# Second mixer of a two-layer trunk: compact inverse in 32-column tiles, mean-free v, decays from running sums, one written order per engine

## Chip, cores and metric

One core of a Trainium2 chip. The metric is the device time of one execution, in microseconds; the runs shown before the change are three of the same program.

## What is computed

A causal two-layer trunk on 512 tokens of width 1024, in f32: layer 0 has a gated linear attention and a spatial gating unit, layer 1 an RWKV-7 time mixing and a Conformer convolution; each layer ends in an output projection and a squared-ReLU MLP. The change is in layer 1. Of the reference, what matters:

```python
# RWKV-7, heads of 64 channels
h = h + (token_shift(h) - h) * mu
r, k, v, xw, xa, xg = split(h)
decay = exp(-exp(-softplus(-(w0 + tanh(xw) @ w2)) - 0.5))
a = sigmoid(a0 + xa @ a2);  g = sigmoid(xg) @ g2
kk = heads(k * k_k);  kk = kk / max(norm(kk), 1e-12)
k = k * (1 + (a - 1) * k_a)
# S_t = S_{t-1} (diag(decay_t) - kk_t^T (kk_t * a_t)) + v_t^T k_t ;  y_t = S_t r_t
y = scan(r, decay, k, v, kk, a)
y = (y - mean(y)) * rsqrt(var(y) + 64e-5) * gn_g + gn_b      # per head
y = (y + sum(r * k * r_k) * v) * g
# Conformer: z = a * sigmoid(gate); 31-tap causal depthwise conv + bias; LayerNorm; silu
```

## The kernel before

Everything is channel-major: a tile holds 128 channels on the partitions and 512 tokens in the columns. f32 matrix products with weights are made of three f32r products: weights and activations are cut into a high part (ScalarE: `w_hi`, line 720 in this stage) and a rest (GpSimd: `w_lo`, line 501), and every one of the eight k-steps of an output tile takes three matmuls of 512 columns (`tile`, line 861). Weights come in chunks of two tiles, double-buffered; SP loads chunk n once the rest of chunk n-2 is made, ScalarE cuts it once TensorE is through with chunk n-2.

The second mixer has 22 input tiles (`ROWS`): 14 go through the token shift (`evac_a`, `evac_q`, `evac_b`: psh by VectorE, dsh by ScalarE, the mix by VectorE into kx, vT, rx, low0 or low1), 8 are values and gates of the convolution. Then four channel blocks c = 0..3 of two heads each, in four time chunks of 128:

- `zw`, `za`: two products of 512 columns give the decay and a. `decay`: a running sum over each chunk (line 1670), the sum less its value at the middle (1673) and less the step itself (1678) by VectorE, three exponentials of 128x512 by ScalarE (739, 742, 744).
- `ksq`, `ks`, `kn`: norm of kk. `dyn`: eight VectorE steps that make AR (two parts: kk and r, decayed), bT and kT. `bonus` (line 1158).
- `scores`: for each of the 8 pairs yy of chunk and head four products in a bank, which VectorE copies under a mask into SC; then the start X, XT of the inverse, and three transposes into vtok, btok, ktok.
- The inverse of a triangular 128x128 matrix for each yy, by doubling: level lv = 1..6 has `tx` (line 1204: SC with one half of X, 64 columns; ScalarE copies it to TX, line 772) and `dx` (line 1219: TX with XT, and 1216: XT with TX; VectorE copies both under masks into X and XT, lines 1756 and 1758). Each is done in two halves b of four yy. X, XT and TX are full 128x128 although only blocks along the diagonal are in use until the last level.
- State, per chunk n: `g` (1234, 1238), `u` (1246), `st` (state 1256 and 1258, output y 1263 to 1267), with copies by ScalarE (G line 777, U line 781) and VectorE (Sp line 1779).
- `post`: y less its head mean (a product with BLK of 512 columns, line 1275, and a VectorE step), variance (1280), root, spread (1288), gain and gn_b by ScalarE, bonus and gate by VectorE.
- `taps`: 31 VectorE steps per block on cv (line 1807), each on the result of the one before; then `conv_ln`, and the output projection `out` (1327), which needs m_hi and m_lo of every block.

The order of all of this is one list, `ORDER1`, made by loops: the slices (quarters of an input tile, two k-steps each) are put between the steps of a block by the tables `FILL`, `SCORE_N`, `LEVEL_N`, `STATE_N`, the taps by `LEVEL_TAPS`, and the evacuation of a tile stands right behind its last slice. Each engine walks through this same list and does its own part of each step; nothing within one engine overtakes. At the start of the kernel, VectorE makes byte masks from `masks_f`.

Of the kernel before, what the change touches and what calls it, by code (L numbers as in the profile page):

```python
# [8 lines left out]
SEQ = 512  # L9
FF = 4 * D  # L10
P = 128
KD = D // P
TT = SEQ // P
# [3 lines left out]
CT = 4  # L17
# [3 lines left out]
COLUMN_HALVES = [slice(0, 64), slice(64, 128)]  # L21

# [29 lines left out]
for _name, _n, _times in [("gla", 128, 2), ("score", 256, 2), ("reset64", 128, 4), ("reset128", 128, 4)] \  # L52
        + [(f"lvl{a}{lv}", 64, 4) for lv in range(LEVELS) for a in ("X", "XT")]:
    MSRC[_name] = (sum(n for _, n in MSRC.values()), _n)
    MCOLS[_name] = (sum(n for _, n in MCOLS.values()), _n * _times)
# [4 lines left out]
def build(nc, xT_in, weights, cols_in, mats_in, masks_in, sgu_ln_in, sgu_w_in, alpha_w_in, low_w_in, out):  # L60
# [5 lines left out]
    with ctx:  # L66
# [24 lines left out]
        before_stages = sb("before_stages", [P, 56])  # L91
# [69 lines left out]
        with ExitStack() as own:  # L161
# [21 lines left out]
            t_a = sb("t_a", [P, SEQ])  # L183
# [5 lines left out]
            zpad = sb("zpad", [P, SEQ + TAPS - 1])  # L189
            sgate = dsh  # L190
# [12 lines left out]
            c_norm = sb("c_norm", [P, TT])  # L203

# [35 lines left out]
        def half_of(t, b, B, side):  # L240

            v = t[:, :, :].rearrange("p y (q h b) -> p (y q) h b", h=2, b=B)
            q = P // (2 * B)
            return v[:, 4 * b * q:4 * (b + 1) * q, side, :]

        def half_of_one(t, yy, B, side):
            return t[:, yy, :].rearrange("p (q h b) -> p q h b", h=2, b=B)[:, :, side, :]

# [36 lines left out]
        DYN = ["at", "ab", "ak", "bt", "k2", "kt", "rt", "rk"]  # L285
        POST = ["yc", "yrs", "yn", "yb", "ym"]
        LN = ["st", "mv", "rs", "scaled", "gain"]

# [42 lines left out]
        def quarters(tiles):  # L331
            return [("slice", t, q) for t in tiles for q in range(4)]

        def taps_in(c, counts):
            ends = [sum(counts[:i + 1]) for i in range(len(counts))]
            return [[("taps", c, e - n, e)] if n else [] for n, e in zip(counts, ends)]

        ORDER1 = [("slice", t, q) for q in range(4) for t in (0, 2)] + [("stat",)] + quarters([4]) + [("spread",)] \
            + quarters([3])[:2] + [("zw", 0)] \
            + quarters([3])[2:] + [("za", 0), ("decay_v", 0, 0), ("ksq", 0)] \  # L340
            + [("decay", 0, 1), ("decay_v", 0, 1)] + quarters([14])[:1] + [("ks", 0), ("ks_v", 0), ("decay", 0, 2)] \
            + [("decay_v", 0, 2), ("kn", 0), ("kn_v", 0)] + quarters([14])[1:] + [("dyn", 0, 0)] \
            + [("dyn", 0, 1)] + quarters([15])[:3] + [("bonus", 0), ("slice", 15, 3)]
        FILL = {0: [5, 7, 6, 1, 16, 17], 1: [8, 10, 9, 18, 19], 2: [11, 13, 12], 3: [20, 21]}

        SCORE_N = {0: [1] * 6, 1: [1] * 6, 2: [1, 1, 1, 1, 0, 1], 3: [2, 2, 1, 1, 1, 1]}
        LEVEL_N = {0: [1] * 6, 1: [1] * 6, 2: [1, 1, 1, 1, 0, 0], 3: [0] * 6}
        STATE_N = {0: [2, 1] * 4, 1: [1] * 8, 2: [1, 0, 1, 0, 1, 0, 0, 0], 3: [0] * 8}
        LEVEL_TAPS = {0: [5, 5, 2, 4, 1, 2, 3], 1: [5, 5, 2, 2, 1, 1, 3], 2: [5, 5, 2, 2, 1, 1, 3],
                      3: [1, 3, 5, 2, 5, 4, 5]}  # L350
        for c in range(CT):
            gaps = quarters(FILL[c])

            def fill(n):
                took = gaps[:n]
                del gaps[:n]
                return took
# [21 lines left out]
            for i in range(6):  # L379
                ORDER1 += [("scores", c, i)] + fill(SCORE_N[c][i])  # L380
# [1568 lines left out]
```

## Time and profile before

| | us |
|---|---|
| median of 3 runs (lowest to highest) | 1389.52 (1388.11 to 1390.04) |
| profiled execution | 1388.51 |
| its span, first to last instruction | 1386.7 |
| busy over the span: PE, PEld | 1279.2, 1038.0 |
| DVE, ACT, POOL | 682.2, 421.6, 518.6 |

PE is TensorE, PEld its weight loads, DVE VectorE, ACT ScalarE, POOL GpSimd. Matmul records overlap and their ends are modelled: what a stream of matmuls costs is read from start to start, and the busy time of a stretch counts overlap once. Idle time is read together with what ended it.

### The profile page before, as it was taken

How to read it: one execution, taken by the hardware profiler on the slowest of the kernel's cores; microseconds unless marked ns; L12 is line 12 of the kernel's file. 1: busy time of each engine (PE TensorE's matmuls, PEld its weight loads, DVE VectorE, ACT ScalarE, POOL GpSimd, SP SyncE). 2: the span in 40 equal slices, each digit the busy share in tenths (PEclk: the TensorE clock that was granted, in tenths of full speed). 3: DMA queues.
4: the chain of work that ended last, by engine and by line, in shares of the span. 5: the costliest groups of instructions: out<-in, count | busy, mean ns of one | idle time of the engine just before them, and what ended most of it. 6: DMA issues, size and time to landing. Idle time of an engine off the chain costs nothing.

```text
span 1386.7 us, 21884 instructions
## 1 busy us (share of the span) xinstructions
PE 1279.2 (92%) x9060; PEld 1038.0 (75%) x9060; DVE 682.2 (49%) x992; ACT 421.6 (30%) x536; POOL 518.6 (37%) x374
## 2 busy tenths in 40 slices
PE   5999999999999999979798888787899999999997
PEld 4797978888888888856666656564688888888885
DVE  7435365551124444457758587675655511244334
ACT  4547333221122222253334324222432211222110
POOL 4341435554445555431121030110245544455541
PEclk9899999999999999989999999897999999999998
DMA  4331212222322223210011010000022232222221
GB/s 183 115 107 46 77 72 96 91 91 100 112 91 91 91 91 105 101 67 32 32 34 50 11 50 14 31 33 1 28 95 91 91 105 108 91 91 91 94 88 61
DMA packets 16808, 105.74 MB, mean 76 GB/s; under 512 B 1872, under 2 KB 2144, under 8 KB 4832
## 3 DMA queue, kind: packets, MB, share of 16 engines
q1 hardware_dynamic: 16304, 104.03, 21.1%
q8 instruction: 58, 0.95, 0.3%
q10 hardware_dynamic: 432, 0.64, 0.1%
q14 instruction: 14, 0.11, 0.0%
HBM read 102.57 MB, written 2.10 MB: 75 GB/s over the span
## 4 chain that ended last, share of the span: by engine, by line
issue 50%; PE 27%; POOL 21%; DVE 1%; DMA 0%; POOLq 0%; ACT 0%; SPq 0%; DVEq 0%
PE ps L861 23%; POOL w_lo L501 21%; PE ps L946 3%; PE ps L915 1%; DMA w_raw<-in_weights 0%; DVE x L1361 0%; PE ps L896 0%; POOL w_lo L490 0%; POOLq L495 0%; ACT w_hi L601 0%; POOLq L498 0%; SPq L454 0%; DVE xsq L1372 0%; DVE scaled L1431 0%; DVE x L1433 0%
## 5 line engine op out<-in xcount | busy, mean ns | idle before, releaser
L501 POOL TENSOR_TENSOR w_lo<-w_raw,w_hi 128x512 fp32r<-128x512 f32 x368 | 509.6, 1415 | 827.5 <-ACT w_hi L514 284.1
L861 PE MATMUL ps<-h_hi,w_hi 128*128 128x512 f32 x696 | 283.7, 408 | 11.6 <-POOL w_lo L490 11.6
L861 PE MATMUL ps<-h_lo,w_hi 128*128 128x512 f32 x696 | 275.0, 395 | 0.0
L861 PE MATMUL ps<-h_hi,w_lo 128*128 128x512 f32 x696 | 274.8, 395 | 0.0
L861 PEld LDWEIGHTS ps<-h_hi,w_hi 128*128 128x128 f32 x696 | 132.8, 191 | 51.3 <-issue 12.2
L589 ACT ACTIVATE w_hi<-w_raw 128x2048 fp32r<-128x2048 f32 x50 | 95.7, 1914 | 194.7 <-PE ps L861 143.4
L861 PEld LDWEIGHTS ps<-h_hi,w_lo 128*128 128x128 f32 x696 | 132.8, 191 | 28.7
L861 PEld LDWEIGHTS ps<-h_lo,w_hi 128*128 128x128 f32 x696 | 133.3, 192 | 25.9 <-issue 0.5
L861 PE MATMUL ps<-f_hi,w_lo 128*128 128x512 f32 x384 | 149.5, 389 | 0.0
L861 PE MATMUL ps<-f_hi,w_hi 128*128 128x512 f32 x384 | 149.5, 389 | 0.0
L861 PE MATMUL ps<-f_lo,w_hi 128*128 128x512 f32 x384 | 149.5, 389 | 0.0
L1403 DVE TENSOR_TENSOR f_hi<-relu 128x512 f32 x64 | 56.8, 888 | 154.7 <-ACT relu L564 152.8
L564 ACT ACTIVATE relu<-ps 128x512 f32<-128x512 f32 x56 | 33.5, 598 | 223.4 <-PE ps L861 223.4
L1807 DVE SCALAR_TENSOR_TENSOR cv<-zpad,cols,cv 128x512 f32<-128x512 f32 x120 | 99.3, 827 | 3.2
L514 ACT ACTIVATE w_hi<-w_raw 128x2048 fp32r<-128x2048 f32 x32 | 61.1, 1909 | 80.0 <-PE ps L861 56.9
L861 PEld LDWEIGHTS ps<-f_hi,w_hi 128*128 128x128 f32 x384 | 72.1, 188 | 15.0
L861 PEld LDWEIGHTS ps<-f_hi,w_lo 128*128 128x128 f32 x384 | 72.1, 188 | 14.9
L1421 DVE TENSOR_TENSOR scaled<-ps,rn 128x512 f32<-128x512 f32 x16 | 11.1, 691 | 146.7 <-PE ps L861 112.1
L861 PEld LDWEIGHTS ps<-f_lo,w_hi 128*128 128x128 f32 x384 | 72.1, 188 | 14.8
L990 PE MATMUL ps<-w_hi,h_hi 128*128 128x256 f32 x256 | 76.4, 298 | 2.7 <-POOL w_lo L493 2.1
L990 PE MATMUL ps<-w_lo,h_hi 128*128 128x256 f32 x256 | 74.0, 289 | 0.0
L990 PE MATMUL ps<-w_hi,h_lo 128*128 128x256 f32 x256 | 73.9, 289 | 0.0
(305 smaller groups left out, 1941.9 us busy)
## 6 DMA issues: line engine op xcount, KB each, us to landing
w_raw<-in_weights SPq DMA_DIRECT2D x93, 1024.0 KB, 4.9
outT<-x SPq DMA_DIRECT2D x8, 256.0 KB, 2.0
x<-in_xT SPq DMA_DIRECT2D x6, 256.0 KB, 7.3
masks_f<-in_masks SPq DMA_DIRECT2D x1, 768.0 KB, 10.6
x<-in_xT ACTq DMA_DIRECT2D x2, 256.0 KB, 5.6
w_raw<-in_weights SPq DMA_DIRECT2D x1, 512.0 KB, 6.4
low_w<-in_low_w SPq DMA_DIRECT2D x1, 512.0 KB, 11.3
sgu_ln<-in_sgu_ln SPq DMA_DIRECT2D x1, 512.0 KB, 3.6
```

The lines of the kernel that those rows point to most:

```text
L501: piece = pool.tensor_tensor(w_lo[:, j, at], w_raw[:, j, at], w_hi[:, j, at].bitcast(f32), SUB)
L514: act.activation(w_hi[:, n % 2, :], w_raw[:, n % 2, :], ACT.Copy).then_inc(s("hi_done"), 1)
L564: act.activation(relu[:, g % 2, :], bank(g % 2), ACT.Relu).then_inc(s("relu_done"), 1)
L589: act.activation(w_hi[:, n % 2, :], w_raw[:, n % 2, :], ACT.Copy).then_inc(s("hi_done"), 1)
L861: mm = pe.matmul(bank(gb(g) if isinstance(i, int) else g % 2), w, r, start=(k == 0 and m == 0), stop=(k == K - 1 and m == 2))
L915: mm = pe.matmul(bank(gb(gu + t)), w, r, start=(k == 0 and m_ == 0), stop=(k == KD - 1 and m_ == 2))
L946: mm = pe.matmul(bank((gd + j) % 2), w, r, start=(k == 0 and m_ == 0), stop=(k == HALF_K - 1 and m_ == 2))
L990: mm = pe.matmul(tok_bank(g), a, b, start=(k == 0 and m == 0), stop=(k == KD - 1 and m == 2))
L1403: tt(f_hi[:, bass.ds(4 * i + c, 1), :].rearrange("p a n -> p (a n)"), relu[:, g % 2, :], relu[:, g % 2, :], MUL).then_inc(s("fhi_done"), 1)
L1421: tt(scaled[:, j, :], bank((gd + j) % 2), rn[:, :], MUL)\
L1807: stt(cv[:, c, :], zpad[:, j:j + SEQ], col("conv_w", TAPS * c + j), cv[:, c, :], MUL, ADD)\
```

## The change

- *Inverse.* X, XT and TX become `xc`, `xtc`, `txc` of 64 columns per yy, which hold only the two 64x64 diagonal blocks. Levels 1 to 5 run as four tiles of 64 rows and 32 columns of weights (`QUARTERS`) with 32 moving columns; `dx` (for X) and `dxt` (for XT) are steps of their own, `dxt` for all eight yy at once; VectorE copies X in halves of 128 columns and XT once per level in 256. Level 6 makes only the block off the diagonal: 64 columns, copied by ScalarE into `txc` and XT; ScalarE also copies the diagonal blocks into XT (`xt_diag`). Banks alternate by level.
- *Scores.* The products of the two heads alternate, so that neighbours use different halves of the partitions.
- *Mean-free v.* v is transposed by a product with `CEN` (identity less the head mean), so y comes out without its mean; the mean product and its step go; gain and gn_b are part of VectorE's steps.
- *Decays.* The running sum has a zero in front of each chunk (129 columns), and ScalarE makes the three exponentials straight from it, in pieces of 128x128 with the middle as bias; t_c's and t_b's VectorE steps go. The step with k_a moves to ScalarE (`ak`, into `t_g`).
- *Room.* Two buffers each for dsh and zpad; the gate uses zpad itself.
- *Order.* `ORDER1` and the loops that make it go. Three lists are written out, `PE1` (443 steps), `DVE1`, `ACT1`, one per engine, with single k-steps for quarters, single taps, `s` and `y` for `st`.
- *Start of the kernel.* The masks have 1025 columns for 1536, made into bytes by 12 steps for 18. The clearing of SC and others stands ahead of the norm.

```diff
-            X = sb("X", [P, 8, P])
             XT = sb("XT", [P, 8, P])
-            TX = sb("TX", [P, 8, P])
+            xc = sb("xc", [P, 8, 64])
+            xtc = sb("xtc", [P, 8, 64])
+            txc = sb("txc", [P, 8, 64])
...
+            def exps(c):
+                act.wait_ge(s("cum_done"), c + 1)
...
+                for dst, first, i, name, last in ((t_b, 0, 0, "ea_done", "at"), (t_c, 1, 1, "en_done", "kt"),
+                                                  (t_d, 1, 0, "ep_done", "rt")):
+                    if c:
+                        act.wait_ge(*dyn_step(last, c - 1))
...
+                    for n in range(TT):
+                        one = act.activation(dst[:, n * P:n * P + P], cum[:, n, first:first + P], ACT.Exp,
+                                             bias=mid[:, i, n:n + 1], scale=(-EXP_HALF, EXP_HALF)[i])
+                    one.then_inc(s(name), 1)
...
+                    for lhs, at in ((bT, slice(0, 256)), (kT, slice(256, 512))):
+                        for h2, r in enumerate(COLUMN_HALVES):
+                            ar = AR[r, c % 2, i, :, :].rearrange("p a n -> p (a n)")
+                            mm = pe.matmul(bank(5 + h2, at.start, at.stop), lhs[r, i * P:i * P + P], ar,
+                                           start=True, stop=True)
...
+                        for r, to in QUARTERS:
+                            mm = pe.matmul(as2(ps[to, tx_bank(lv, b), 32 * at:32 * at + 32], B), SC[r, yy, to],
+                                           side_of_one(xc, r, yy, B, 0), start=True, stop=True)
...
+                        for r, to in QUARTERS:
+                            w = slice(to.start - r.start, to.stop - r.start)
+                            mm = pe.matmul(as2(ps[to, x_bank(lv, b), 32 * at:32 * at + 32], B), xtc[r, yy, w],
+                                           side_of_one(txc, r, yy, B, 0), start=True, stop=True)
...
+            def dxt(c, lv):
...
+                for yy in range(8):
+                    for r, to in QUARTERS:
+                        w = slice(to.start - r.start, to.stop - r.start)
+                        mm = pe.matmul(as2(ps[to, xt_bank(lv), 32 * yy:32 * yy + 32], B), txc[r, yy, w],
+                                       side_of_one(xtc, r, yy, B, 1), start=True, stop=True)
...
+                    if b == 0:
+                        mm = pe.matmul(to, one, CEN[:, :], start=True, stop=True)
...
-                    pe.matmul(bank(7), BLK, y[:, :], start=True, stop=True).then_inc(s("ymean_mm"), 1)
...
-                    tt(t_c[:, :].rearrange("p (n t) -> p n t", t=P), b3, b3[:, :, 63:64].broadcast_to([P, TT, P]), SUB)\
...
-                    tt(t_b[:, :], t_c[:, :], t_a[:, :], SUB).then_inc(s("ca_done"), 1)
```

A stretch of the new list of TensorE, block 3, which has no slices left:

```diff
+            ("scores", 3, 4), *run("slice", 21, 5, 8), ("conv_mean", 0), *run("tok_tr", 3, 0, 3), ("tx", 3, 1, 0),
+            ("tx", 3, 1, 1), ("dx", 3, 1, 0), ("dx", 3, 1, 1), ("dxt", 3, 1), ("tx", 3, 2, 0), ("tx", 3, 2, 1),
+            ("post", 2, 0), ("dxt", 3, 2), ("dx", 3, 2, 0), ("dx", 3, 2, 1), ("tx", 3, 3, 0), ("tx", 3, 3, 1),
...
```

## Rows read from the trace of the kernel before

**Rows 1.** Stretches: length; busy time of PE, PEld, DVE, ACT, POOL; clock, DMA share, GB/s.
```profile
576.20:629.00 52.80, 42.81 (x239) 32.14 (x237) 26.75 (x50) 23.11 (x32) 15.96 (x12) 0.90 0.20 73
629.00:719.90 90.90, 78.37 (x977) 58.60 (x976) 62.33 (x100) 30.71 (x57) 16.80 (x12) 0.94 0.10 36
719.90:808.80 88.90, 76.31 (x1005) 55.82 (x1003) 64.17 (x100) 31.10 (x57) 18.10 (x12) 0.94 0.11 37
808.80:891.80 83.00, 66.13 (x957) 47.59 (x955) 62.10 (x100) 29.52 (x55) 11.16 (x8) 0.92 0.08 25
891.80:963.40 71.60, 57.10 (x883) 42.50 (x884) 50.20 (x88) 18.70 (x40) 4.99 (x4) 0.93 0.05 18
963.40:989.00 25.60, 21.57 (x242) 15.93 (x238) 8.97 (x17) 10.04 (x17) 0.00 (x0) 0.80 0.00 1
...
629.00:645.20 16.20, 15.95 (x113) 11.22 (x112) 11.12 (x18) 6.49 (x10) 5.00 (x4) 1.00 0.18 66
911.40:941.20 29.80, 22.06 (x599) 18.84 (x598) 26.10 (x48) 9.36 (x20) 4.99 (x4) 1.00 0.11 37
```

**Rows 2.** Waits of PE, second mixer: us in total, times, longest.
```profile
PE ps L1204 <- DVE XT L1758: 22.0, 21, 5.7
```

**Rows 3.** Timeline before the first score product: start us, us, engine and line, [idle before].
```profile
614.13 0.75 DVE L1691 SCALAR_TENSOR_TENSOR t_f<-kx,cols,ps 128x512 f32<-128x512 f32 x1 [2.14 <-PE ps L1152]
620.52 0.69 DVE L1631 TENSOR_TENSOR dsh<-rn,ps 128x512 f32<-128x512 f32 x1 [5.64 <-PE ps L861]
...
626.56 1.13 PE L1158 MATMUL ps<-rx,mats 128*128 128x512 f32 x2 [1.99 <-DVE rx L1721]
```

**Rows 4.** Timeline of PE, short products, K*M of the weights, columns.
```profile
629.01 0.71 PE L1172 MATMUL ps<-AR,bT 64*128 64x256 f32 x4
...
639.81 0.70 PE L1178 MATMUL ps<-bT,AR 64*64 64x64 f32 x32
640.44 0.50 PE L861 MATMUL ps<-h_hi,w_hi 128*128 128x512 f32 x1
...
641.01 0.39 PE L861 MATMUL ps<-h_hi,w_lo 128*128 128x512 f32 x1
641.24 0.40 PE L861 MATMUL ps<-h_hi,w_hi 128*128 128x512 f32 x1
...
645.21 1.16 PE L1204 MATMUL ps<-X,SC 128*64 128x64 f32 x32
646.30 1.12 PE L1130 MATMUL ps<-low,low_w 32*128 32x512 f32 x2
...
648.94 0.34 PE L1216 MATMUL ps<-TX,XT 128*64 128x64 f32 x4
...
650.76 0.29 PE L1219 MATMUL ps<-XT,TX 128*64 128x64 f32 x4
...
751.28 0.43 PE L1280 MATMUL ps<-mats,ysq 128*32 128x2 f32 x32
751.64 0.50 PE L861 MATMUL ps<-h_hi,w_hi 128*128 128x512 f32 x1
```

**Rows 5.** Groups of VectorE, second mixer: busy us, mean ns | idle before.
```profile
L1807 DVE SCALAR_TENSOR_TENSOR cv<-zpad,cols,cv 128x512 f32<-128x512 f32 x120 | 99.3, 827 | 3.2
...
L1758 DVE COPY_PREDICATED XT<-masks,ps 128x256 f32<-128x256 uint8 x48 | 22.9, 483 | 0.6 <-PE ps L1219 0.6
...
L1756 DVE COPY_PREDICATED X<-masks,ps 128x256 f32<-128x256 uint8 x40 | 20.0, 500 | 27.5 <-PE ps L1219 27.5
```

**Rows 6.** Groups of ScalarE, second mixer.
```profile
L742 ACT ACT_TABLE_LOAD x4 | 5.1, 1283 | 0.1
...
L777 ACT ACTIVATE G<-ps 128x128 f32<-128x128 f32 x16 | 4.4, 274 | 46.9 <-PE ps L1238 46.9
...
L815 ACT ACTIVATE cv<-cv,cols 128x512 f32<-128x512 f32 x4 | 2.9, 802 | 0.0
...
L827 ACT ACTIVATE m_hi<-ym 128x512 fp32r<-128x512 f32 x4 | 2.5, 620 | 0.0
```

More of the change, by code:

```diff
@@ L21 @@
 COLUMN_HALVES = [slice(0, 64), slice(64, 128)]
+QUARTERS = [(h, slice(a, a + 32)) for h in COLUMN_HALVES for a in (h.start, h.start + 32)]
 MIX0 = [1, 4, 4, 2, 2, 4, 4, 4, 4, 4, 4]
@@ L326, in build @@
         TOK = {"v": (v_tok, 1), "sv": (sv, 5), "u": (u_tok, 7), "g": (g_tok, 9)}
[L331 to L343, printed above, removed]
@@ L399, in build, with run @@
[L399 to L403 removed]
+        def run(name, *a):
+            return [(name, *a[:-2], k) for k in range(a[-2], a[-1])]
@@ L1317, in out_, with conv_mean, conv_var @@
-            def out_(t, a, b):
-                n, g = N_OUT1, FIRST_TILE[N_OUT1] + t
-                if a == 0:
+            def conv_mean(c):
+                pe.wait_ge(s("tap_done"), TAPS * (c + 1))
+                if c == 0:
+                    pe.wait_ge(s("score_done"), 8 * CT)
+                mm = pe.matmul(bank(6), ONES, cv[:, c, :], start=(c == 0), stop=(c == CT - 1))
+                if c == CT - 1:
+                    mm.then_inc(s("cmean_mm"), 1)
+            def conv_var(c):
+                pe.wait_ge(s("csq_done"), c + 1)
+                if c == 0:
+                    pe.wait_ge(s("conv_step"), CT)
+                for n in range(TT):
+                    for q in range(0, P, 32):
+                        mm = pe.matmul(ps[q:q + 32, 6, n:n + 1], (t_f, t_b, t_d, t_e)[c][:, n * P + q:n * P + q + 32],
+                                       ONES[:, 0:1], start=(c == 0 and n == 0), stop=(c == CT - 1 and n == TT - 1))
+                mm.then_inc(s("cvar_mm"), 1)
@@ L1328, in out_ @@
-                if b == KD:
+                k = M_TILES[i]
+                pe.wait_ge(s("m_lo_done"), 8 + i + 1)
+                for m, (w, r) in enumerate(cuts(n % 2, t * KD + k, k, M_HI1[k], M_LO1[k])):
+                    mm = pe.matmul(bank(g % 2), w, r, start=(i == 0 and m == 0), stop=(i == KD - 1 and m == 2))
+                if i == KD - 1:
                     mm.then_inc(s("gemm_done"), 1)
             steps = {"slice": slice_, "stat": lambda: stat(2), "spread": lambda: spread(2), "zw": zw, "za": za, "ks": ks, "kn": kn,
-                     "bonus": bonus, "scores": scores, "tx": tx, "dx": dx, "g": g_, "u": u_, "st": st, "post": post, "conv_ln": conv_ln, "out": out_}
@@ L1663, in decay @@
[L1663 to L1681 removed]
+                    dve.wait_ge(s("psh_zero"), 1)
@@ L1827, in m @@
                 tt(M_LO1[k], M_SRC1[k], F(M_HI1[k]), SUB).then_inc(s("m_lo_done"), 1)
-            steps = {"stat": start, "spread": started, "evac_a": evac_a, "evac_b": evac_b, "decay_v": decay, "ks_v": ks, "kn_v": kn, "dyn": dyn, "bonus": bonus, "scores": scores,
-                     "dx": dx, "st": st, "post_v": post, "taps": taps, "conv_ln": conv_ln, "m": m}
-            for name, *a in ORDER1:
+            steps = {"stat": lambda: norm(2), "zero": zero, "evac_a": evac_a, "evac_b": evac_b, "scan": scan, "dec": dec_,
+                     "ks_v": ks, "kn_v": kn, "dyn": dyn, "bonus": bonus, "scores": scores, "dx": dx, "dxt": dxt, "s": s_,
+                     "post_v": post, "tap": tap, "conv_sub": conv_sub, "conv_root": conv_root, "conv_scale": conv_scale, "m": m}
+            for name, *a in DVE1:
                 if name in steps:
```

847 lines of the change are left out of this document (490 added, 357 removed), and 27 rows, old and new, of tables (ACT1, PE1).

## The prediction

> **What bounds the kernel now.** I read three kinds of view, in this order. First the table of stretches [rows 1]: the second mixer runs from 576.2 to 989.0 us of a span of 1386.7 us, 412.8 us, and the change touches next to nothing outside it. The columns to look at are those of TensorE (busy 42.81, 78.37, 76.31, 66.13, 57.10 and 21.57 us, 342.3 together), of VectorE (274.5) and of ScalarE (143.2), and the granted clock, under 1.00 in all six stretches. So TensorE is the bound, but an imperfect one: for 70.5 us it stands, and in part of the rest it is at 1.2 GHz, the lower of its two levels. The cuts are the first score product of each channel block (629.0, 719.9, 808.8, 891.8), the last state product (963.4) and the last step of `out` (989.0).
>
> Second, for whom TensorE waits [rows 2]: 22.0 us in 21 waits go to L1204 (`tx`, the first product of a level) behind L1758, VectorE's last copy of the level before. Why such a copy is late is seen in the timeline [rows 3]: after t_f at 614.13 VectorE stands for 5.64 us, since the next step in the one common order is the evacuation of tile 14 (L1631); the eight steps of `dyn` behind it could have run, and the bonus product comes only at 626.56. The order sets this, no resource does.
>
> Third, the timeline of the short products [rows 4]. An f32 product leaves two records. `tx` takes 1.09 us for both halves (645.21 to 646.30), the 64 records of `dx` 1.94 us (648.94 to 650.88, 0.12 us for each group of four), one f32 product of 512 columns 1.12 us with its drain (646.30). A matmul of a slice follows the last after 0.23 us (641.01, 641.24), so a k-step is 0.68.
>
> **TensorE, part by part.** (a) *Compact inverse.* Now five levels of 1.09 + 1.94 and a last one with half the `dx`, 2.06: 17.2 us a block, 69 us in four. After: 64 + 64 + 64 records a level, 64*32 tiles with 32 columns, 960 in five levels; the last level has 64 records with 64 columns on two column tiles. No row has 64*32 with 32 columns. From above: L1178, four tiles of 64*64 with 64 columns, 32 records in 0.63 us (639.81 to 640.44), 19.7 ns. From below: a quarter of the 29 ns of a `dx` record, half the columns on twice the tiles, 7.3 ns. L1280 has the width of 32 and four column tiles, but 2 columns: 32 records in 0.36 us (751.28 to 751.64), 11.3 ns [rows 4]. It is the nearest, so I take 12 ns: 11.5 us, plus 64 x 0.029 = 1.9, is 13.4 us a block. Saved: 3.8 us a block, 15 in four; by the bounds from 33 saved to 14 lost.
>
> Records with 2 columns start 11.3 ns apart and those with 64 columns 19.7 ns [rows 4]. Against this change speaks the Trainium skill, TensorEngine Tiling (Array Packing), Performance Considerations: one column takes as long as 60, and no tiling factor should be taken from a dimension that is small already. The two rows do not bear that out for four tiles side by side, and by L1280's row the time is 1313.7; by the page it would be that of the second rival, 1343.
>
> (b) *Scores.* The first four records of a pair of heads take 0.71 us with their drain (629.01), all eight 1.07. With the two halves of the partitions in turn they can run two at a time. I take 0.86 (between 0.53 and 1.07): 0.2 x 16 = 3.4 us saved. (c) *Mean-free v.* Four 512-column mean products over y go, 4 us; the centring rides on transposes of v that are there anyway. (d) *Finer steps.* Counted in the two orders, slices stand in 65 unbroken runs before and in 65 after, so changes between the two kinds of product cost the same.
>
> **The other engines.** VectorE [rows 5]: t_c, t_b, t_e and one step on y go, sixteen steps like the 0.69 of L1631 [rows 3], 11 us. X copies go from 256 to 128 columns: 40 x 0.50 becomes 40 x 0.35 (between 0.25 and 0.50), 6 us. XT copies of the same size fall from 48 to 20, at 0.483: 13.5 us. Level 0 saves 1. Together 31 us: 274.5 becomes 243, 55 to 60 of it in each block. ScalarE [rows 6]: three exponentials per block in 12 pieces of 128x128 at 0.274 (3.3 us), for three steps of 128x512 like the 0.620 of L827 (1.9 us); t_g, two diagonal and two last copies of XT, +2.6; smaller level copies and the two steps on y that go, -2. That is 2 us a block more; it stays the idlest of the three, but its queue matters: the writer of t_b, t_c and t_d waits for at, kt and rt of the block before, and behind it stand `tx` copies for which TensorE waits at `dx`. POOL's work per chunk is unchanged (67.0 busy of 412.8), and its weights come as before, per chunk. At the start of the kernel the masks shrink (512 KB for 768, 12 casts for 18). Nothing in the first products reads them; I take 0. Six casts fewer, none dearer than the 0.483 of L1758, would save up to 3 us if nothing hid them, and a layout that moves costs 1 at most.
>
> **The sum, stretch by stretch.** Each is TensorE's new work over the share in which it is busy, or VectorE's, or the chain, whichever is longest. TensorE's share is 86% in block 0 now and 98% where slices stand between all short steps (629.0 to 645.2) [rows 1]; I take 92%. VectorE is at 88% at its densest (911.4 to 941.2), and I take that. The few us "from the clock" are a choice: at 0.93 to 0.94 some 10 us of a block are at the lower level, and shorter waits give part of them back.
> - Up to the first score: TensorE has 46 k-steps of 0.68 and 6 us of short work, 37 us. In the chain to the bonus product `spread` comes six k-steps sooner (4 us), the 5.64 us go, one table load of 1.28 us goes, the exponentials cost 1.4 more, and t_c and t_b go (1.4). That is 11 us, and one more for the hand-overs of the steps that go; 52.8 becomes 41.
> - Block 0: 78.4 - 3.8 - 0.9, + 0.7 (51 k-steps for 50), - 2 from the clock: 72; over 0.92, 78 for 90.9.
> - Block 1: 76.3 - 3.8 - 0.9 - 1.0, + 2.7 (44 k-steps for 40), - 2: 71; 77 for 88.9.
> - Block 2: 66.1 - 5.7 - 2 = 58; 63 for 83.0. VectorE, 62.1 - 8 = 54 over 0.88, 61, is just under it.
> - Block 3: 11 k-steps for 16, and VectorE binds: 50.2 - 8 + 5 (six taps of block 2 fall here now, 0.827 each) = 47; over 0.88, 53, and some 5 from the last tap to the last state product: 58 for 71.6.
> - Tail: y 1.5; square and copy 1.2; variance, root, reciprocal 0.9; a table 1.28; four silu and cuts of 0.80 + 0.61, 5.6; the last cut and rest 1.3; six matmuls 1.6; hand-overs 1: 14.5. With out steps that come late, 20 for 25.6.
>
> 41 + 78 + 77 + 63 + 58 + 20 = 337 for 412.8: 75.8 us less, of which 22 are work and the rest waiting and clock. The profiled execution took 1388.51 us, 1.8 of it outside the span; the median of 1389.52 lies 1.0 above it, so 1389.5 - 75.8 = 1313.7.
>
> **Rivals.** *The waits stay.* The new lists are fixed; if steps end later than they were written for, each in-order queue hands its delay on and TensorE idles as now. Then only the work goes: 1389.5 - 22.4 = 1367. For it: the three queues have to agree through 443 steps of TensorE alone. Against it: today's idle times are at places that the new lists visibly fill. 12%.
> *The tiles give nothing.* A record of 32 columns holds its tile as long as one of 64, so it costs the 19.7 ns of L1178: 14 us lost for 15 saved, 1343. For it: both ends of my bound have 64 columns; against it: L1280. 7%. It is the rule of TensorEngine Tiling (Array Packing) in the Trainium skill.
> *Denser than I take.* 98% everywhere and a clock near 1.00: 315 us for the stage, 1292. 10%.
> *Slower.* `exps` is one block of 12 x 0.274 us, three small ones and a table load, 5.2 us in ScalarE's queue between `tx` copies, with cuts of the weights beside it, while TensorE stands at `dx` in its own fixed order. The mean wait at `tx` is 22.0/21 = 1.05 us now, the longest 5.7 [rows 2]. With 24 levels the gain is gone from 3.2 us of added waiting a level on; at 3.5 it is 1389.5 - 75.8 + 84 = 1398. Only three such blocks stand inside levels: 3%.
>
> **Numbers.** The forecast has 68% (its own bounds: 1297 to 1339), the rivals 12, 7, 10 and 3. The range of 1294 to 1346 leaves out the first rival, the last, and half of the denser one, 20%. About 0.2% (2.8 us) is what a measurement of this kernel can tell from no change: faster 0.96, same 0.01, slower 0.03.
>
> **What would show it.** A stage near 337 us in which TensorE idles 30 to 40 us; records of `tx`, `dx` and `dxt` some 12 ns apart (20 by the second rival); under 10 us of waits at `tx`; VectorE and not TensorE dense in block 3; the bonus product of block 0 near 614. I am wrong if TensorE still idles 70 us, if VectorE's copies of 128 columns cost what those of 256 do, if ScalarE becomes what TensorE waits for most, or if a stage outside the second mixer moves by more than 1 us.

## The result, and the profile after

The changed kernel takes 1351.59 us (median of 4 runs, 1345.29 to 1354.03) where the kernel before takes 1389.47 (1388.11 to 1390.04) beside it: a ratio of 0.9717, 95% interval 0.9696 to 0.9738. Its profiled execution took 1352.92 us, with a span of 1351.1. I had said 1313.7, with 1294 to 1346 as the range. The gain is 38 us where I had put 76: the sign was right, the size was half, and the range missed.

The table of stretches of the changed kernel, cut as [rows 1]: first score product of each block, last state product, end of the stage. Columns: length, then busy time and records of TensorE, its weight loads, VectorE, ScalarE and GpSimd, the granted clock, DMA share, GB/s. The last line is the whole stage.

```profile
core 0: us, PE busy (x) PEld busy (x) DVE busy (x) ACT busy (x) POOL busy (x), PEclk, DMA share, GB/s
577.30:619.30 42.00, 40.03 (x233) 29.82 (x231) 22.90 (x51) 25.33 (x44) 12.88 (x11) 0.96 0.18 67
619.30:707.20 87.90, 73.58 (x1433) 54.06 (x1433) 50.98 (x87) 29.65 (x66) 18.14 (x14) 0.90 0.15 50
707.20:790.50 83.30, 74.23 (x1534) 52.46 (x1532) 53.68 (x95) 35.58 (x78) 12.35 (x10) 0.98 0.08 28
790.50:860.40 69.90, 59.17 (x1405) 42.72 (x1402) 41.50 (x75) 26.37 (x63) 8.14 (x7) 0.85 0.10 33
860.40:937.60 77.20, 60.57 (x1520) 43.32 (x1518) 51.88 (x90) 21.27 (x48) 10.88 (x8) 0.73 0.09 30
937.60:953.20 15.60, 15.60 (x107) 11.85 (x104) 9.12 (x16) 8.72 (x13) 0.00 (x0) 0.91 0.01 2
...
577.30:953.20 375.90, 323.19 (x6217) 234.23 (x6215) 230.06 (x412) 146.92 (x311) 62.40 (x48) 0.88 0.11 38
```

The stage takes 375.9 us for 412.8; I had 337. Block 3 is the odd one: 77.2 us, longer than the 71.6 of before [rows 1], at a granted clock of 0.73, where I had forecast 58. TensorE's work fell by 19.1 us and its idle time from 70.5 to 52.7. I had written that it would idle 30 to 40 us; the 337 itself leaves room for some 23 only (342.3 of work, less 22.4 saved, less 6 for the clock, is 314).

Who TensorE waits for, over the stage (us in total, times, longest). At the head of this view of before stood steps of other engines. Behind the 22.0 us of [rows 2] came:

```profile
PE ps L1152 <- DVE k_norm L1687: 9.7, 4, 4.7
PE ps L1256 <- ACT U L781: 8.9, 7, 5.0
PE ps L1234 <- DVE Sp L1779: 8.1, 9, 3.0
```

In the changed kernel:

```profile
PE ps L1397 <- issue: 14.4, 9, 3.0
PE ps L1381 <- issue: 7.9, 7, 1.8
PE ps L1359 <- issue: 5.2, 3, 2.3
PE ps L1425 <- ACT G L905: 3.0, 8, 0.4
PE ps L992 <- issue: 2.9, 1, 2.9
PE ps L1413 <- DVE Sp L1985: 2.6, 5, 0.6
PE ps L1464 <- issue: 2.4, 1, 2.4
```

The waits for other engines, on which my whole argument turned, are as good as gone: the largest is 3.0 us. In their place stand 33 us of "issue", time in which TensorE waits for nothing that the profile shows: at L1397 (`dxt`), L1381 (`dx`), L1359 (`tx`), at L992, a weight slice whose operands had long been there, and at L1464 (the sum of squares in `post`). By engine, the named waits are 10.9 us for ScalarE and 7.0 for VectorE; before they were 18.7 and 51.9.

Two of these pieces in the timeline of TensorE in block 0 (start, length, what, and in brackets the idle time ahead of it), with two groups that run without a pause ahead of them:

```profile
640.67 0.76 PE L1397 MATMUL ps<-xtc,txc 64*32 64x32 f32 x64
641.28 0.41 PE L1381 MATMUL ps<-txc,xtc 64*32 64x32 f32 x26
...
645.68 0.46 PE L1381 MATMUL ps<-txc,xtc 64*32 64x32 f32 x32
645.96 0.48 PE L1397 MATMUL ps<-xtc,txc 64*32 64x32 f32 x32
648.70 0.64 PE L1397 MATMUL ps<-xtc,txc 64*32 64x32 f32 x30 [2.25 <-issue]
649.10 0.24 PE L1359 MATMUL ps<-xc,SC 64*32 64x32 f32 x1
649.10 0.24 PE L1397 MATMUL ps<-xtc,txc 64*32 64x32 f32 x2
649.15 1.05 PE L1359 MATMUL ps<-xc,SC 64*32 64x32 f32 x63
650.16 0.65 PE L1381 MATMUL ps<-txc,xtc 64*32 64x32 f32 x32
653.76 0.79 PE L992 MATMUL ps<-h_hi,w_hi 128*128 128x512 f32 x1 [2.95 <-issue]
```

The first piece lies in the middle of one step: `dxt` issues its 64 records with no wait among them, and 32 run before the pause and 32 behind it. Between the two pauses run 30 + 1 + 2 + 63 + 32 = 128 records. The trace has 127 weight loads and one entry of the sequencer beside them, 256 instructions together. The table of DMA queues has a queue of kind "instruction" (packets, MB, share). In the changed kernel, over the stage and over 880 to 912 us, the levels of block 3:

```profile
q8 instruction: 49, 0.80, 0.9%
...
q8 instruction: 9, 0.15, 2.0%
```

In the kernel before, over the stage and over 907 to 941 us, the levels of its block 3:

```profile
q8 instruction: 33, 0.54, 0.5%
...
q8 instruction: 5, 0.08, 0.9%
```

Each packet has 16384 bytes. TensorE's records and weight loads in the stage are 6217 + 6215, 12432 (with 206 entries of its sequencer 12638), and 12638/49 is 258 a packet; before, 4289 + 4286 + 85 = 8660 over 33 is 262. So a packet is some 256 instructions of TensorE. In the stretch of the first timeline packets start at 642.2, 646.1, 651.6 and 655.0 us: the two pauses begin at 646.4 and 650.8. Of the 34.0 us in 18 idle pieces of over 0.8 us in the stage, 29.2 us in 14 begin within 1.2 us of the start of such a packet; before, it was 16.7 of 53.9 us, and each of those four pieces had a named step of another engine behind it. The end of a pause says more than its start. Sixteen of the 18 pieces (31.4 us) are "issue", and every one of them ends 2.2 to 2.7 us after a packet starts. So do all 135 such pieces of the changed kernel and the 14 runs below (2.2 to 3.0 us); the kernel before has none. In block 3, which has most of the pauses, the packets are 3.3 to 3.9 us apart (5.4 us between the two at the pauses shown above), and in no run of this case is any pair closer than 3.2 us. That is 13 to 15 ns an instruction, an estimate from this spacing. The compact inverse issues 192 records and 192 loads a level, where the old one had 96 and 96 (32 of `tx` [rows 4] and 64 of `dx`), and a record with its load now takes 9.5 ns at the full clock (64 of them from 640.67 to 641.28): 1.2 us for 128 records, for which a packet takes 3.3.

The Trainium skill, Runtime: NRT & Kernel Launch, section Instruction fetch mechanics, has the instructions refilled in blocks of 16 KiB, 256 of them, and calls the cost "mostly hidden". This trace agrees on the block (16384 bytes a packet) and not on the cost (31.4 us in this stage).

### The profile page after: what moved, and what is told of

Same layout as the page of the kernel before. It is cut to its first block, busy times and chain, and to the rows that moved or that the text cites. A ratio compares the mean times of both kernels' runs of the same rounds, so it can differ in the third digit from the quotient of the medians.

```text
span 1351.1 us, 26048 instructions
## 1 busy us (share of the span) xinstructions
PE 1260.3 (93%) x10988; PEld 1020.0 (75%) x10988; DVE 634.3 (47%) x950; ACT 425.4 (31%) x592; POOL 513.9 (38%) x374
## 4 chain that ended last, share of the span: by engine, by line
issue 49%; PE 28%; POOL 21%; DVE 1%; DMA 0%; POOLq 0%; ACT 0%; SPq 0%; DVEq 0%
PE ps L992 23%; POOL w_lo L572 21%; PE ps L1077 3%; PE ps L1046 1%; DMA w_raw<-in_weights 0%; DVE x L1549 0%; PE ps L1027 0%; POOL w_lo L561 0%; POOLq L566 0%; ACT w_hi L672 0%; POOLq L569 0%; SPq L525 0%; DVE x L1621 0%; DVE scaled L1619 0%; DVE xsq L1560 0%
## 5 line engine op out<-in xcount | busy, mean ns | idle before, releaser
L992 PE MATMUL ps<-h_hi,w_hi 128*128 128x512 f32 x696 | 284.1, 408 | 14.7 <-POOL w_lo L561 11.6
L992 PE MATMUL ps<-h_lo,w_hi 128*128 128x512 f32 x696 | 275.1, 395 | 0.0
L992 PE MATMUL ps<-h_hi,w_lo 128*128 128x512 f32 x696 | 274.7, 395 | 0.0
L992 PEld LDWEIGHTS ps<-h_hi,w_hi 128*128 128x128 f32 x696 | 132.9, 191 | 50.3 <-POOL w_lo L561 11.6
L992 PEld LDWEIGHTS ps<-h_hi,w_lo 128*128 128x128 f32 x696 | 132.9, 191 | 28.7
L992 PEld LDWEIGHTS ps<-h_lo,w_hi 128*128 128x128 f32 x696 | 133.2, 191 | 25.9 <-issue 0.7
L992 PE MATMUL ps<-f_hi,w_hi 128*128 128x512 f32 x384 | 149.4, 389 | 0.0
L992 PE MATMUL ps<-f_lo,w_hi 128*128 128x512 f32 x384 | 149.4, 389 | 0.0
L992 PE MATMUL ps<-f_hi,w_lo 128*128 128x512 f32 x384 | 149.4, 389 | 0.0
L2012 DVE SCALAR_TENSOR_TENSOR cv<-zpad,cols,cv 128x512 f32<-128x512 f32 x120 | 90.6, 755 | 2.7
L992 PEld LDWEIGHTS ps<-f_hi,w_hi 128*128 128x128 f32 x384 | 72.1, 188 | 15.1
L992 PEld LDWEIGHTS ps<-f_lo,w_hi 128*128 128x128 f32 x384 | 72.1, 188 | 14.9
L992 PEld LDWEIGHTS ps<-f_hi,w_lo 128*128 128x128 f32 x384 | 72.1, 188 | 14.9
L1121 PE MATMUL ps<-w_hi,h_hi 128*128 128x256 f32 x256 | 76.4, 298 | 3.7 <-POOL w_lo L564 3.1
L1121 PE MATMUL ps<-w_lo,h_hi 128*128 128x256 f32 x256 | 74.0, 289 | 0.0
L1121 PE MATMUL ps<-w_hi,h_lo 128*128 128x256 f32 x256 | 73.9, 289 | 0.0
```

Of the source, the lines that this page charges most:

```text
L992: mm = pe.matmul(bank(gb(g) if isinstance(i, int) else g % 2), w, r, start=(k == 0 and m == 0), stop=(k == K - 1 and m == 2))
L1121: mm = pe.matmul(tok_bank(g), a, b, start=(k == 0 and m == 0), stop=(k == KD - 1 and m == 2))
L2012: stt(cv[:, c, :], zpad[:, c % 2, j:j + SEQ], col("conv_w", TAPS * c + j), cv[:, c, :], MUL, ADD)\
```

## The experiments

All kernels are variants of the changed kernel; the ratio of each is to the kernel before, measured beside it. "Pieces" are idle pieces of TensorE of over 0.8 us in the stage. The expectations set these accounts against each other: A, TensorE waits for its instructions; B, the idle time is hand-overs between engines and the lower clock that small products bring; C, VectorE sets the length of block 3; D, the clock is a cause of its own beside A. Times are medians, but stretches, clocks and pieces come from the one profiled execution, which was the slowest of four in e5 (1341.3 us) and e6 (1349.2) and the fastest in e4 (1340.1) and e13 (1344.1).

**Half the records, everywhere** (e1_halves), in short form:

```
-  for r, to in QUARTERS:          # tiles of 64*32, four side by side
-      matmul(ps[to, ...32 columns], SC[r, yy, to], side(xc))
+  for r in COLUMN_HALVES:         # tiles of 64*64, two side by side
+      matmul(ps[r, ...32 columns], SC[r, yy, r], side(xc))
   (dx, dxt and the last level alike)
```

> Theory A, instruction supply: in the changed kernel TensorE's idle pieces of 1.0 to 3.0 us (16 of them, 31 us) each begin within 0.7 us of the start of a 16 KB packet of the instruction queue, and 49 such packets fall in the second mixer where there were 33. Here tx, dx and dxt use stationary tiles of 64*64 with the same 32 columns instead of 64*32: same result, half the records (256 products a block fewer, with two records and two weight loads each, 4096 instructions in all, 16 packets of 256). Expected: 33 packets, hardly an idle piece over 1 us without a semaphore behind it, block 3's granted clock from 0.73 back to 0.9 or more; 1318 to 1332 us. Theory B, clock and hand-overs: the idle time is the chain tx, copy, dx, copy and the lower clock that small products bring. Then nothing is gained by fewer records; with two tiles side by side instead of four the records start 20 to 29 ns apart instead of 13, the inverse takes 46 to 68 us instead of 61, and the time is 1343 to 1359. Theory C, VectorE sets block 3: 1345 to 1352.

1336.2 us, ratio 0.9643 (0.9590 to 0.9695). The instruction queue is back at 33 packets, the pieces fall from 34.0 to 4.2 us, all idle time from 52.7 to 21.1:

```profile
577.30:937.40 360.10, 339.04 (x4157) 256.22 (x4156) 231.88 (x408) 146.98 (x311) 62.73 (x48) 0.91 0.11 37
```

Who TensorE waits for, at the head of this kernel's list:

```profile
PE ps L1423 <- ACT G L905: 3.0, 8, 0.4
PE ps L1411 <- DVE Sp L1983: 2.6, 5, 0.6
PE ps L1431 <- ACT U L912: 1.9, 5, 0.4
```

Theory B (nothing gained from fewer records) and C fall: work went up and the time went down. The time lies 4 us above the range that I had for A: the records now start 38 ns apart on average, so that the levels' work went from 61 to 84 us, 23 us more against the 32 us of idle time saved; all work of the stage rose by 15.8.

**The same, with narrow products in place of the records saved** (e2_halves_narrow). In front of each group 16, 32 or 8 records of 2 columns on 128*32 tiles, into unused columns.

> The run before it, with as many products of 2 columns on tiles of 128*32 put in front of each group of tx, dx and dxt as the wider tiles had saved (256 a block, 1024 in all, into unused columns of the group's own bank; the output stays the same). They cost 11.3 ns a record by their row, 23 us if they all lie on the path. Theory A: 49 packets of instructions again, idle pieces of 1 to 3 us in the middle of groups come back, 25 to 35 us over the run before, of which over 15 us is idle time and not work. Theory B: the work alone, 15 to 23 us, evenly, with no idle piece in the middle of a group.

1399.1 us, ratio 1.0070 (1.0036 to 1.0104): 63 us over the run before, and neither theory has that. There are 49 packets again, as close as 3.3 us, but the pieces did not come back (2.8 us). The time is in the records: the narrow ones take 34 us (16.8 ns each), the level records went from 38 to 49 ns, and the lower clock stands for 123 us of the stage where it was 68. So the sign that I had named for A, pauses in the middle of groups, failed to appear. A reason can be worked out afterwards: the records of these levels, narrow ones included, start 34 ns apart on average (140.6 us for 4096), 4.4 us for 128 of them, and that is slower than the packets came where TensorE stood. The run says that instructions for nothing are dear here; how much of it is supply it can't tell.

**Work for nothing in block 3** (e3_fill_block3): two products of 128x512 behind each of its 29 groups, 116 instructions.

> The changed kernel, with two f32r products of 512 columns behind each of the 29 groups of tx, dx and dxt of block 3, into a bank that nothing uses there (58 products, 0.23 us each, 13.3 us of work at the full clock, 116 instructions). Theory A: they run while the next instructions are on their way; block 3 has 13.7 us of such idle time and 40 us at the lower clock, so it loses at most 3 us and may win up to 6; the packets of the instruction queue lie as close as before (3.6 to 3.9 us) except that the time between them is now work. Theory B, the clock is the cause: the granted clock of block 3 goes from 0.73 to over 0.95 and the block falls by 5 to 10 us in spite of the added work. Theory C, VectorE sets block 3: no change. If each product adds its 0.23 us, the block grows by 13 us and all three fall.

1348.2 us, ratio 0.9715 (0.9681 to 0.9749), as the changed kernel. Block 3 took 76.1 us for 77.2 although 19.4 us of work (335 ns a product) had been put in:

```profile
857.80:933.90 76.10, 68.65 (x1576) 44.70 (x1576) 54.12 (x90) 21.27 (x48) 10.89 (x8) 0.99 0.09 30
```

Its clock is 0.99. The idle pieces of the block fell from 11.3 to 2.1 us. So about as much as was put in had been lost there, to pauses and to the lower clock together. An unchanged time was also what theory C had; this run doesn't tell A from C, the next one does.

**VectorE** (e4_no_taps_block3): 30 of 31 taps of the last block work on one element, so that this part of the convolution is left out (in short form):

```
+  if c == CT - 1 and j:
+      ts(cv[0:1, c, 0:1], cv[0:1, c, 0:1], 1.0, None, MUL)   # for the tap of 128x512
```

> The changed kernel, in which 30 of the 31 taps of the last block's convolution are replaced by an operation on a single element (that part of the convolution is left out; its order and its hand-overs stay). It takes 30 x 0.7 us, 20 us, from VectorE in block 3. Theory C, VectorE sets block 3: the block falls from 77 us by 12 to 18 us. Theory A (instruction supply) and B (clock and hand-overs): the 26 us of levels don't move, and only the end, where the mean of the convolution waits for the last tap, comes earlier: 0 to 6 us.

1345.0 us, ratio 0.9695 (0.9661 to 0.9728). Block 3 lost 15.6 us of VectorE's work and 4.6 us of its length (72.6). VectorE doesn't set it, against what my forecast had: at most the end of it.

**Only the order** (e5_spread): 23 of 176 slices moved in TensorE's list, most of them out of runs of 4 to 10, to places between the steps of the levels ahead; not one instruction more or less. Block 0 as an example:

```
-  ("dx",0,1,1), ("tx",0,2,0), ("slice",7,3), ("tx",0,2,1), ("dx",0,2,0), ("ks",1), ("dx",0,2,1), ("dxt",0,2),
+  ("dx",0,1,1), ("slice",7,4), ("tx",0,2,0), ("slice",7,5), ("tx",0,2,1), ("dx",0,2,0), ("slice",7,6), ("ks",1),
+  ("dx",0,2,1), ("slice",7,7), ("dxt",0,2), ("slice",6,0),
```

> The changed kernel with 23 of the 176 weight slices moved in TensorE's written order, from the runs of 4 to 10 in blocks 0 to 2 to places between the steps of the levels ahead of them; no instruction is added or left out. A slice gives TensorE 0.68 us of work for 6 instructions, a level's group 0.4 us for 64. Theory A, instruction supply: of the nine idle pieces at fetches ahead of block 3 (20.0 us) 8 to 16 us go, 1336 to 1344, with 49 packets as before and block 3 as before. Theory B, hand-overs: the same steps with the same waits, and the slices put ahead only delay the chain of levels: 1350 to 1360.

1334.5 us, ratio 0.9606 (0.9578 to 0.9635), 17 us under the changed kernel. 49 packets as before, the pieces 23.2 us for 34.0, most of the difference in blocks 0 and 1; block 0 fell from 87.9 to 82.2 us:

```profile
617.70:699.90 82.20, 75.14 (x1433) 52.71 (x1433) 52.62 (x87) 29.70 (x66) 18.94 (x14) 0.96 0.15 54
```

This run is the cleanest for supply: same instructions, same work, same waits, and slices (0.68 us for 6 instructions) put where 64 instructions were going by in 0.4 us. Theory B had 1350 to 1360. Not all of the 17 us is shown to be supply. Between the two profiled executions the stage is 11.6 us shorter, and 10.5 of that is idle time; the other three executions of e5, 5 to 11 us faster than the profiled one, also had a higher mean clock (0.972 to 0.974 for 0.962).

**64*64 tiles in block 3 alone** (e6_whole_block3).

> 64*64 tiles (half the records) in block 3 alone, the narrow tiles in blocks 0 to 2. In block 3 no slice stands between the levels, so supply is worst there: 13.7 us of idle pieces at fetches and 44 us at the lower clock. With 64*64 tiles everywhere, block 3 and the tail together took 77.6 us for 92.8. Theory A: the same here, 1335 to 1341. Theory B', that the run with 64*64 tiles won through something else in blocks 0 to 2: 1348 to 1356, since a record costs 38 ns for 13 and block 3's inverse 6 us more.

1344.1 us, ratio 0.9683 (0.9661 to 0.9705): 7.5 us under the changed kernel, 3 short of what I had. The pauses of block 3 are gone (one of 1.0 us left, behind a copy), yet it takes 77.3 us, where the same instructions took 63.4 in e1. The two profiles differ in the granted clock, and e6's is that of its slowest execution, 5 us above its median. Block 3 of e1 in the table of stretches:

```profile
859.80:923.20 63.40, 56.15 (x1010) 42.18 (x1006) 53.48 (x89) 21.12 (x48) 10.90 (x8) 0.92 0.09 29
```

And of e6:

```profile
858.20:935.50 77.30, 71.14 (x1008) 55.20 (x1006) 52.17 (x89) 21.07 (x48) 10.88 (x8) 0.69 0.08 29
```

**Out steps earlier** (e7_whole_block3_out) and **all three** (e8_spread_whole3_out): `m` 0 and 1 on ScalarE and VectorE and four k-steps of `out` moved from the tail to between block 3's levels; then with e5's order.

> The run before it, and the first two k-steps of both tiles of the out product (4 x 0.7 us), with the two cuts that they need on ScalarE and VectorE, moved from the tail to between the levels of block 3. TensorE is dense in the tail (15.8 of 15.8 us), so 1.5 to 3 us less than the run before; if the two cuts (0.6 and 0.7 us each) delay the copies of the levels by as much, no gain.

> The three together: slices spread in blocks 0 to 2, 64*64 tiles in block 3, out steps early. If the three are separate gains of instruction supply and order they add up: 1351.6 less 8 to 16, less 11 to 16, less 1 to 3: 1317 to 1332. If they share one cause outside supply, no better than the best of the three by more than 2 us.

1347.6 (0.9715, 0.9693 to 0.9738) and 1339.0 us (0.9620, 0.9557 to 0.9682). The first is no gain over e6, the second none over e5: the three don't add up. That is the outcome that I had put down for a cause outside supply. In e8 the pieces are down to 15.8 us, and block 3, at a clock of 0.73, takes 79.1.

**Is the clock a cause of its own?** e9_spread_fill puts 17 products of 128x512 for nothing into block 3 of e5, e10_whole_block3_fill puts 11 into the 64*64 form of it.

> The kernel with spread slices (narrow tiles everywhere; median 1334.5) and one f32r product of 512 columns, for nothing, behind the first tx, the first dx and the dxt of each level of block 3, 17 in all. In that kernel's profile block 3 took 73.2 us at a mean granted clock of 0.81, 27 us of it at the lower level, with 10 us of idle pieces at fetches. Theory D, the clock is a second cause beside supply: it falls where TensorE stands for instructions and then makes the work dearer; the 17 products (up to 5.7 us of work, most of it in the idle pieces) hold it at 0.95 or more and the block falls to 64 to 69 us, the time to 1326 to 1331. Theory A alone, supply and nothing else: the products hide in the idle pieces, the block stays within 2 us, 1333 to 1337. If they simply add up: 1339 to 1341.

> Spread slices, 64*64 tiles in block 3, and one such product for nothing behind the second dx and the dxt of each of its levels, 11 in all. The same code of block 3 took 63.3 us in one profile at a granted clock of 0.92 and 77.3 in another at 0.69, both with no idle piece of over 1 us at a fetch in it. Theory D, the clock is a cause of its own: with it held at 0.95 the block takes 63 plus at most 3.7, the time is 1323 to 1330. If the clock is not what tells those two profiles apart: 75 to 80 us and 1335 to 1341.

1338.5 (0.9620, 0.9583 to 0.9657) and 1338.7 us (0.9623, 0.9566 to 0.9679): neither is where theory D had it, and e10 is where I had it if the clock is not what tells e1 from e6. But the clock, which they were to hold up, wasn't held. With 17 the clock of block 3 rose from 0.81 to 0.89 only and the block went from 73.1 to 76.1 us; with 11 it stood at 0.78 and the block at 77.3. The products neither hold the clock nor are free (494 and 650 ns each), so these two runs decide nothing on D.

> As the run with 64*64 tiles in block 3 and 11 products for nothing (1338.7; its block 3 took 77.3 us at a clock of 0.78, 34 us at the lower level), with 29 of them, one behind every group of tx, dx and dxt. Theory D, the clock decides between the 63.3 and the 77.3 us that the same 64*64 code took: with a product behind every group it stays at 0.95 or more, and the block takes 63 plus 29 x 0.23 to 0.33, 70 to 73 us; 1329 to 1334. If it is something else: 77.3 plus 4 to 6, 81 to 84 us; 1341 to 1345.

e13_whole3_fill29 has one behind all 29 groups. Its median is 1357.3 us (ratio 0.9779, 0.9731 to 0.9828), over both of my ranges, so it is no version to keep. Its profiled execution took 1344.1 us and had a mean clock of 0.975; the other three took 1356.7 to 1365.9 at 0.955 to 0.961. In that profile block 3's clock was 0.98, the block 74.3 us, 1.3 over my range, with 12.7 us of it (438 ns a product) in the products for nothing:

```profile
785.00:855.10 70.10, 58.50 (x1402) 40.92 (x1400) 40.97 (x75) 26.28 (x62) 6.12 (x5) 0.91 0.10 33
855.10:929.40 74.30, 68.75 (x1037) 47.70 (x1035) 53.90 (x89) 21.13 (x48) 10.92 (x8) 0.98 0.07 24
```

**64*64 tiles in blocks 2 and 3** (e14_whole23), with e5's order: does a long block 2 make block 3 short?

> Spread slices, 64*64 tiles in blocks 2 and 3. It asks whether block 3 was short (63.3 us) in the run with 64*64 tiles everywhere because block 2 ahead of it was long (76.5 us for 70), which gives VectorE time to be ahead with the taps. If that is so, block 2 takes 73 to 77 us and block 3 62 to 66 at whatever clock, and the sum of the two is 137 to 142 us for 146 to 147 with 64*64 tiles in block 3 alone. If the clock decides: block 3 takes 63 where its clock is over 0.9 and 73 to 78 where it is under 0.8, and the sum can be as high as 150.

1330.7 us, ratio 0.9561 (0.9523 to 0.9600), the fastest of all, 21 us under the changed kernel. Blocks 2 and 3:

```profile
777.20:854.80 77.60, 74.17 (x893) 55.67 (x890) 41.49 (x75) 26.36 (x63) 8.15 (x7) 0.76 0.08 29
854.80:917.90 63.10, 55.67 (x1008) 41.68 (x1006) 53.49 (x89) 21.13 (x48) 10.92 (x8) 0.95 0.08 28
```

By itself this can't choose: block 2 was long and the clock of block 3 was high. e13's profile speaks for the clock. There block 2 took 70.1 us, so VectorE had no head start, and without the 12.7 us for nothing block 3 would be 61.6 us at a clock of 0.98. This is an estimate from one execution, and takes every product as lying on the path. By it the 64*64 block takes 62 to 63 us at 0.92 to 0.98 and 77 at 0.69, whatever block 2 did. The price of a group of 32 records at either level is in the timelines, of e14 at 2.4 GHz:

```profile
877.07 1.10 PE L1421 MATMUL ps<-xtc,txc 64*64 64x32 f32 x32
878.01 1.10 PE L1383 MATMUL ps<-xc,SC 64*64 64x32 f32 x32
```

And of e6 at 1.2:

```profile
884.63 1.92 PE L1402 MATMUL ps<-xtc,txc 64*64 64x32 f32 x32
886.36 1.90 PE L1386 MATMUL ps<-txc,xtc 64*64 64x32 f32 x32
```

0.94 us from one group to the next, and 1.73. Executions of one kernel point the same way: e8's took 1324.4 us at a mean clock of 0.982 and 1338.7 to 1341.0 at 0.968.

**Two small prices.** e11_spread_wide_sums makes the sums over heads with 128*128 tiles, 576 instructions fewer; e12_no_centring turns v with the plain transpose, so that the mean of y over a head is not taken out.

> The kernel with spread slices (1334.5), in which the sums over the channels of a head (k_norm, y_norm) and of the convolution's variance are made with stationary tiles of 128*128 instead of 128*32: 32 records become 8, twelve times, 576 instructions fewer in all (2.25 packets of 256). A record of 128*32 with 2 columns starts 11.3 ns after the last; one of 128*128 has a weight load of 190 ns by the rows of the slices, unless it overlaps. Theory A: 1 to 4 us less, 1330 to 1334, if the loads overlap; 1335 to 1339 if each of the 96 records costs 60 ns or more on the path.

> The changed kernel (1351.6) with v turned by a plain transpose as before, so that the mean of y over a head is not taken out at all (that part of the computation is left out). It prices the product with the centring matrix: 32 records, 3.88 us in four blocks, where the transposes are 16 records, 1.80 us. Expected 2 us less, 1349 to 1351, in every theory; the clock moves single runs of this kernel by up to 8 us, so that no more than 'not over 5 us' can be read.

e11: 1337.1 us (0.9610, 0.9566 to 0.9653), in the upper of my two ranges but not to be told from e5. e12: 1341.6 us (0.9656, 0.9619 to 0.9693), 10 us under the changed kernel and not 2. Its records and packets stay nearly the same (49), its pieces are 30.0 us for 34.0, and its lower clock stands for 68 us for 89. So 2 us are the records, some 4 are pauses, and the rest goes with the clock; that the 16 records fewer brought the clock up was not shown. So a change of next to nothing in TensorE's instructions can come with 10 us, and differences of that size between the runs above (e6's 7.5 us among them) are no measure of supply by themselves; the idle pieces are a better one.

## Why the prediction was half right

*The waits for other engines* (it was right, and more than right). I said that the lists would take the waits at `tx` under 10 us. There are 5.2 us at L1359, "issue", and 1.4 us in total behind copies. Without the pauses the stage idles about 21 us, under the 23 of my sum. The first rival, that the waits stay, was wrong.

*The inverse's work* (right in the difference). 15 us saved was the term; summed from start to start, `tx`, `dx` and `dxt` and the last level went from 76.7 to 61.0 us, 15.7 less. My sums had 69 and 54, so both ends were 7 us low, and that they cancel was luck. A record starts 9.5 ns after the last at 2.4 GHz and 13 on average, and the row that I took as nearest (L1280, 11.3 ns [rows 4]) was the right one. The second rival's price, 19.7 ns, was wrong, but its mechanism was not. I had set a row with 2 columns against one with 64 and put the difference down to the columns; the two rows also differ in the width of the weights, 32 and 64. A product of the changed kernel has the 64*64 tiles of L1178 with 32 columns for 64:

```profile
629.07 0.67 PE L1316 MATMUL ps<-bT,AR 64*64 64x32 f32 x32
629.67 0.50 PE L992 MATMUL ps<-h_hi,w_hi 128*128 128x512 f32 x1
```

That is 18.7 ns a record for 19.7: half the columns gave 1 ns, and half the width of the weights then gave the step from 18.7 to 9.5. The Trainium skill has the first of these (TensorEngine Tiling (Array Packing), Performance Considerations): one column takes as long as 60. Those two prices agree with it.

*Three terms of work mis-sized.* The scores saved 1.4 us and not 3.4. The centring product is an f32 product of two records where a transpose leaves one: 3.88 us for 1.80, 2.1 us that I had priced at nothing. The convolution's mean took 6.7 us for 4.3, most of it at the lower clock.

*The step that failed* is the one from work to time: "Each is TensorE's new work over the share in which it is busy". I took 92% from two stretches, 86% and 98%, where the levels' records took 29 ns or more or there were none, and left out that the change brings such a record to 9.5 to 13 ns and raises TensorE's instructions from 8660 to 12638. The count was in my own part (a): 64 + 64 + 64 records a level, for the 32 + 64 of before. I used it for time alone. So the wait for instructions stood at nothing in the sum, and it measured 31.4 us. In blocks 0, 1 and 2 the share was 84, 89 and 85%, and they took 87.9, 83.3 and 69.9 us for my 78, 77 and 63. Block 3, which I had given to VectorE, took 77.2 for 58, half of the miss. The queue of instructions in the trace of before had 33 packets, no two closer than 4.1 us, none of them waited for: enough to ask what a denser stream would do, but no bound. That came with the changed kernel: at 3.3 to 3.9 us a packet, the nine packets in the densest levels of block 3 are 30 to 35 us by estimate, and those levels took 32.

*The clock* (wrong in sign). I had 2 us given back in each of blocks 0 to 2 by shorter waits. The lower level stands for 89 us of the stage and stood for 65 before. In block 3 it falls at 885.9, behind the first pause and 0.1 us into the second, and up to 930.3 it is back for 3.4 us only; e6 and e14, at 0.69 and 0.95, differ by 14 us in the 64*64 form of the block.

*VectorE binds block 3* (wrong). It was to be dense at 88%. In block 3 it is busy 51.9 of 77.2 us, and e4 took 15.6 us of it away for 4.6. Its work came out at 230 us, 13 less than my 243, mostly since a tap now takes 755 ns for 827 [rows 5]. I had not forecast that, and it was luck.

*The rest* (right in the main). The first stretch 42.0 us for 41; the bonus product of block 0 at 617.5 for 614; copies of 128 columns 324 ns for my 350; ScalarE 146.9 us for 151; the tail 15.6 for 20. Two signs that I had named against me did come. ScalarE is now the engine for which TensorE waits most (10.9 us for VectorE's 7.0), though both are small beside the pauses. Ahead of the stage 1.1 us were added (577.3 for 576.2 us), just over what I had called a sign against me; two of TensorE's waits at the start of the kernel (L1104, L1121) are 1 us longer each. I didn't try what does it.

The sum of the miss in the stage, 38.9 us: 29.6 are idle time (52.7 for 23), and 31.4 us of pauses cover that; 9.3 are work (323.2 for 314), of which 6.5 are the three terms above, one of them the clock's. The remaining 3 us I can't assign; the 6 us that the clock was to give back are more than that.

What stays open: why the clock falls in one block and not in another. In e1 and e14 it is low for 37.5 us at one go in block 2, and then for 7 to 10 us in block 3; in e6, e8 and e10 it is low for 24, 7 and 17 us in block 2 and then for 48, 41 and 34 us at one go in block 3. Products for nothing behind all 29 groups held it, 11 and 17 did not. What TensorE did just before it fell was, in each, the start of the levels: the transposes, waits of 0.3 to 0.8 us for ScalarE's copies, and groups of 64*64 tiles. In e1 and e14 a product of 512 columns (`za`) stood among them, in e10 three of those for nothing.

## What to carry to other kernels

Count instructions as you count work. Each f32 product is four of them, and in no run here did a dense stretch of several packets go faster than one packet of 256 instructions in 3.2 us (3.3 to 3.9 where TensorE stood). Where a stretch would be shorter than that, fewer and wider tiles beat faster narrow ones (e1, 15 us). That the narrow ones win where instructions are not short was not shown: their levels are 61 us of work for 84, but no run set the two against each other in time there. Where a dense stretch has to be, put long products between its groups, not behind them: 23 moved slices came with 17 us, some 11 of it idle time. And a forecast of "work over busy share" holds only for records like those the share was read from.

## What the runs showed of the chip that I had not expected

- TensorE pauses for instructions for 1.0 to 3.0 us in the changed kernel (up to 4.3 in e7), some of them in the middle of a group without a wait; the profile calls it "issue". All 135 such pieces end 2.2 to 3.0 us after the start of a packet. Its packets of 256 instructions were never closer than 3.2 us in any run.
- f32 products of 64*32 tiles with 32 columns, four tiles side by side: 9.5 ns from record to record at 2.4 GHz. 64*64 tiles with 32 columns, four side by side: 18.7 ns. The same tiles, two side by side: 30 ns at 2.4 GHz, 54 at 1.2.
- The same block of short products took 63 us at a granted clock of 0.92 to 0.95 and 77 at 0.69, and single executions of one kernel differ by 17 to 20 us (e8: 1324 to 1341, e2: 1390 to 1410), the faster ones at the higher mean clock.
- A product of 128x512 put between groups of short ones takes 335 ns (e3) to 650 ns (e10), and not the 0.23 us that it takes among its like.
